# Conditioning blocks in buffers of their own, 24 of them in the mixer's projections, and two eight-product pairs in three of four feed-forward layers

## The chip, the cores and the metric

The kernel runs on one core of a Trainium2 chip. The metric is the device time of one execution, in microseconds (us); less is better.

## What is computed

One inference step of a two-layer (DEPTH 2) diffusion trunk over T = 640 tokens, 128 of context and 512 latent, with D = 1024 channels, all in fp32:

```python
m = silu(cond) @ ada_w[l] + ada_b[l]                  # 9 vectors of D per layer, two streams
x += 0.5 * m[2] * swiglu_a(modulate(norm(x), m[0:2]))
x += m[5] * mixer_l(modulate(norm(x), m[3:5]))        # even l: attention; odd l: retention
x += 0.5 * m[8] * swiglu_b(modulate(norm(x), m[6:8]))
swiglu(h): a, b = split(h @ w13); (silu(a) * b) @ w2  # w13: 1024 x 2*2816, w2: 2816 x 1024
```

So there are four feed-forward networks, FFN 0 to FFN 3, with mixer 0 (neighbourhood and latent attention over one input projection) between FFN 0 and 1, and the retention mixer between FFN 2 and 3. The two streams (context, latent) have conditioning vectors of their own, so each row of `m` is made twice, from two rows silu(cond).

## The kernel before, in words

Channels lie on the 128 partitions, tokens along the free axis. Every fp32 product is made of three matmuls of fp32r parts (high x high, high x low, low x high), so each weight and each activation needs a high part (rounded, on ScalarE, ACT) and a low part (the difference, on VectorE, DVE).

**Weights.** Blocks of 128 x 1024 (512 KB) or 128 x 768 stream from HBM through the ring `raw` of four slots, in the order that `stream_order()` writes out; the SP queue issues them all (L621). ACT and DVE split a block (`split(n)`: L795 or L802, and L1298) into the two slots of `w2` that TensorE (PE) reads.

**Conditioning.** `ada_w` has 16 groups of KD = 8 blocks of 128 x 1024 that are worked during the run, 128 in all (two further groups are worked at the start). For each, DVE makes a reduction with the silu(cond) row of each stream, `crow[:, s, :]` (L1311, two operations of 1024 columns and a read of each accumulator into `acol`). After each group of eight `ada_out` adds the bias and counts `ada_ev`. These blocks go through the same ring (L623, issued by SP). ADA_UP and ADA_DN say after which tile pair and after which of an FFN's closing tiles how many are worked: 48 in FFN 0, 24 in FFN 1, 24 in FFN 2; 32 come one by one in the retention mixer's heads.

**An FFN.** 22 tile pairs f (an up and a gate tile of 128 channels each) in rounds of 6, 6, 6 and 4; after each round eight "down" tiles add the round's share of the product with w2 (L2171, 288 matmuls a round of six). A pair has one of two forms. The eight-product form (f < CLASSIC[q], `first_pairs`) is 96 matmuls of 320 columns (L2054; the first pair of an FFN is L2100). The seven-product form (`seven_products`) makes the 2 x 2 block product in seven passes of 12 matmuls, 84 in all (L2138). It needs sums of weight quarters (on DVE L1438, L1445, L1452, L1458, with low parts in L1472 and L1467, all `left_low` and `left_..._sum`) and, once for an FFN, sums of activation quarters: the T sums (`t_values` L1481 to L1490, `t_high` on ACT, `t_low` L1500 on DVE), made at pair T_PAIR[q]. Between its passes PE waits for banks of PSUM that ACT (L945, copies to `swu`) and DVE (L1612) have to empty.

**Mixer 0.** Its projections are the steps e = 0 to 13, each with one weight block split two steps ahead (L1761) and in the first eight a memset (L1764); then come two memsets of `va_e`, the norms `nvar` (L1769, L1770), a power on GpSimd (POOL), and `diag` (L1335), which PE needs at L2118. The activations `h2`, `qz` and the rest of the mixer fill SBUF otherwise.

**Names.** raw: ring of weight blocks. crow: silu(cond) rows. acol: accumulators. mod: the finished vectors m. swu: copies of PSUM in a seven-product pair. e2s, e2: T sums and their parts. h2: activations, high and low. n: number of a block; u, r: pair within its round, round.

## Time and profile before

| | |
|---|---|
| median of three runs | 3091.01 us (3086.54, 3091.01, 3091.66) |
| the profiled execution's own time | 3088.77 us |
| its span in the trace | 3086.9 us |
| granted TensorE clock over the span, as a share of 2.4 GHz | 0.988 |
| PE busy | 2953.0 us, 96% |
| DVE busy | 2004.9 us, 65% |
| ACT busy | 1135.0 us, 37% |
| DMA | 294.42 MB, mean 95 GB/s |

A share of busy time is a mean over the stages. The page's chain of waits follows back from the last instruction what released what: here 83% of it lies on PE, 8% on DVE. In the views of single instructions a row is the start, the duration, the engine, the line of the kernel and the operation with out<-in; in brackets stands the idle time of that engine just before it, and the instruction or transfer that ended it.

### The profile page before, as it was taken

How to read it: one execution, taken by the hardware profiler on the slowest of the kernel's cores; microseconds unless marked ns; L12 is line 12 of the kernel's file. 1: busy time of each engine (PE TensorE's matmuls, PEld its weight loads, DVE VectorE, ACT ScalarE, POOL GpSimd, SP SyncE). 2: the span in 40 equal slices, each digit the busy share in tenths (PEclk: the TensorE clock that was granted, in tenths of full speed). 3: DMA queues.
4: the chain of work that ended last, by engine and by line, in shares of the span. 5: the costliest groups of instructions: out<-in, count | busy, mean ns of one | idle time of the engine just before them, and what ended most of it. 6: DMA issues, size and time to landing. Idle time of an engine off the chain costs nothing.

```text
span 3086.9 us, 46070 instructions
## 1 busy us (share of the span) xinstructions
PE 2953.0 (96%) x18222; PEld 2719.1 (88%) x18222; DVE 2004.9 (65%) x3616; ACT 1135.0 (37%) x2024; POOL 275.8 (9%) x335
## 2 busy tenths in 40 slices
PE   7999998998999899999899999999999999999998
PEld 3999898988878899998899998778686886899998
DVE  3778878246756787776787776463635545667766
ACT  4223434335455243444343444222212222534433
POOL 1000002011003000003000003030302104100001
PEclk9999999999999999999999999999999999999999
DMA  5453342220102333332334232312223241122221
GB/s 220 137 175 119 112 128 97 81 70 27 42 15 62 124 112 117 97 113 65 123 104 127 94 107 86 123 62 96 96 76 116 77 129 42 43 94 85 78 82 66
DMA packets 87686, 294.42 MB, mean 95 GB/s; under 512 B 10512, under 2 KB 14896, under 8 KB 86704
## 3 DMA queue, kind: packets, MB, share of 16 engines
q1 hardware_dynamic: 80080, 269.70, 27.0%
q10 hardware_dynamic: 6176, 16.54, 1.4%
q0 software_dynamic: 1216, 5.24, 0.5%
q8 instruction: 144, 2.36, 0.3%
q14 instruction: 70, 0.57, 0.1%
HBM read 283.96 MB, written 7.49 MB: 94 GB/s over the span
## 4 chain that ended last, share of the span: by engine, by line
PE 83%; DVE 8%; ACT 3%; issue 2%; POOL 2%; DMA 1%; DVEq 0%; POOLq 0%; ACTq 0%; SPq 0%
PE ps L2138 23%; PE ps L2171 18%; PE ps L2304 12%; PE ps L2039 11%; PE ps L2054 7%; PE ps L2100 2%; PE ps L2576 2%; POOL tmp_q L644 2%; PE ps L2585 2%; PE ps L2361 1%; PE ps L2329 1%; PE ps L2564 1%; PE ps L2344 1%; PE ps L2252 1%; DVE prod L1311 1%
## 5 line engine op out<-in xcount | busy, mean ns | idle before, releaser
L2171 PE MATMUL ps<-g,w 128*128 128x320 f32 x4224 | 625.0, 308 | 0.6 <-DVE x L1422 0.6
L2171 PEld LDWEIGHTS ps<-g,w 128*128 128x128 f32 x4224 | 620.6, 187 | 1.4 <-issue 0.8
L2138 PE MATMUL ps<-h,w 128*128 128x320 f32 x3168 | 497.5, 312 | 40.7 <-ACT swu L945 28.2
L2138 PEld LDWEIGHTS ps<-h,w 128*128 128x128 f32 x3168 | 474.7, 189 | 45.7 <-ACT swu L945 29.3
L1298 DVE TENSOR_TENSOR w<-raw,w 128x1024 fp32r<-128x1024 f32 (+1 forms) x267 | 302.8, 1140 | 223.4 <-ACT w L795 207.0
L2304 PE MATMUL ps<-w,h 128*128 128x512 f32 x1620 | 374.4, 391 | 4.8 <-ACT rv L1234 3.1
L2138 PE MATMUL ps<-e,w 128*128 128x320 f32 x2376 | 370.6, 309 | 0.0
L2304 PEld LDWEIGHTS ps<-w,h 128*128 128x128 f32 x1620 | 302.3, 188 | 70.0 <-issue 6.8
L2138 PEld LDWEIGHTS ps<-e,w 128*128 128x128 f32 x2376 | 355.0, 188 | 0.0
L808 ACT ACTIVATE w<-w2s 128x512 fp32r<-128x512 f32 x264 | 163.4, 631 | 253.4 <-DVE w2s L1445 71.7
L2054 PE MATMUL ps<-h,w 128*128 128x320 f32 x1728 | 254.3, 309 | 0.2 <-DVE w L1298 0.2
L2054 PEld LDWEIGHTS ps<-h,w 128*128 128x128 f32 x1728 | 253.6, 188 | 0.4 <-issue 0.4
L644 POOL TENSOR_TENSOR tmp_q<-tmp_q 128x320 f32<-128x320 f32 (+1 forms) x66 | 80.3, 1217 | 1744.2 <-ACT tmp_q L838 1738.8
L802 ACT ACTIVATE w<-raw 128x768 fp32r<-128x768 f32 (+1 forms) x144 | 130.7, 914 | 266.1 <-PE ps L2171 202.7
L2039 PE MATMUL ps<-h,w 128*128 128x320 f32 (+1 forms) x1440 | 217.2, 311 | 3.1 <-DVE rk L1925 3.1
L2039 PEld LDWEIGHTS ps<-h,w 128*128 128x128 f32 x1440 | 213.0, 188 | 5.5 <-issue 5.1
L1422 DVE SCALAR_TENSOR_TENSOR x<-ps,gate,x 128x128 f32<-128x128 f32 x224 | 112.1, 545 | 162.5 <-PE ps L2171 145.0
L795 ACT ACTIVATE w<-raw 128x1024 fp32r<-128x1024 f32 x123 | 128.5, 1061 | 231.7 <-PE ps L2039 128.2
L1472 DVE TENSOR_TENSOR w<-w2s,w 128x512 fp32r<-128x512 f32 x264 | 179.0, 684 | 1.1
L1311 DVE CUSTOM_DVE_ANT_0 raw<-raw,crow 128x1024 f32<-128x1024 f32 x128 | 158.0, 1235 | 4.4
L1311 DVE CUSTOM_DVE_ANT_0 prod<-raw,crow 128x1024 f32<-128x1024 f32 x128 | 156.0, 1219 | 5.7 <-ACT crow L884 2.0
L813 ACT ACTIVATE w<-raw 128x512 fp32r<-128x512 f32 x198 | 123.4, 625 | 97.4 <-PE ps L2171 72.8
(246 smaller groups left out, 3376.2 us busy)
## 6 DMA issues: line engine op xcount, KB each, us to landing
raw<-in_ws SPq DMA_DIRECT2D x303, 512.0 KB, 3.6
raw<-in_ada SPq DMA_DIRECT2D x128, 512.0 KB, 3.8
raw<-in_ws SPq DMA_DIRECT2D x96, 384.0 KB, 3.2
ada<-in_ada ACTq DMA_DIRECT2D x6, 1024.0 KB, 22.5
rst<-in_state ACTq DMA_DIRECT2D x4, 1024.0 KB, 4.8
out_new_state<-rsx ACTq DMA_DIRECT2D x8, 512.0 KB, 2.6
x<-in_xT SPq DMA_DIRECT2D x4, 640.0 KB, 8.5
ada<-in_ada POOLq DMA_DIRECT2D x2, 1024.0 KB, 16.7
```

Source lines behind the costliest of these rows:

```text
L644: pool.tensor_tensor(acc_sq, acc_sq, new_sq, ALU.add).then_inc(sq_add, 1)
L795: act.activation(w2[:, slot_of(n), 0, :], raw_of("w", n), ACT.Copy).then_inc(wt_hi, 1)
L802: act.activation(w2[:, slot_of(n), 0, 0:cols], raw_of("w", n)[:, 0:cols], ACT.Copy).then_inc(wt_hi, 1)
L808: act.activation(left(q, f, m, 0), left_value(q, f, m), ACT.Copy).then_inc(left_hi, 1)
L1298: dve.tensor_tensor(w2[:, slot, 1, 0:cols], raw_of("w", n)[:, 0:cols], w2[:, slot, 0, 0:cols].bitcast(fp32), ALU.subtract).then_inc(wt_lo, 1)
L1311: dve.tensor_tensor_reduce(raw_of("a", b) if s else prod0, raw_of("a", b), crow[:, s, :], 1.0, 0.0, ALU.mult, ALU.add, acol[:, k, s:s + 1] ...
L1472: dve.tensor_tensor(lo, left_value(q, f, m) if m else quarter(n, 0), hi, ALU.subtract).then_inc(left_lo, 1)
L2039: mm = pe.matmul(pair_half(pr, half, width), w2[:, slot, wi, at:at + cols], rhs(k, ri)[:, half * width:(half + 1) * width], start=(k == 0 ...
L2054: mm = pe.matmul(pair_half(pr, half), w2[:, slot_of(n), wi, k * P:(k + 1) * P], h2[:, k, ri, half * HT:(half + 1) * HT], start=(k == 0 and ...
L2138: mm = pe.matmul(ps[:, 4 * s + bank, 0:HT], w2[:, at // 2, wi, c:c + P], rhs(k, ri), start=start and k + wi + ri == 0, stop=(k == 3 and wi ...
L2171: mm = pe.matmul(pair_half(pr, half), w2[:, slot_of(n), wi, c:c + P], half_of(g2[:, k, ri, :], half), start=k + wi + ri == 0, stop=(k == n ...
L2304: mm = pe.matmul(ps[:, bank_of(t), :], ones_tile(src(k, ri), t), w2[:, slot_of(n), wi, kk * 512:(kk + 1) * 512], start=(k == 0 and ri == 0 ...
```

## The change

The conditioning blocks of the four FFNs and of mixer 0 leave the weight ring. They get two buffers, `cond0` and `cond1` (in mixer 0 the two halves of `cond_em`), and are loaded by the POOL queue (`condition_load`), each once the block two before it has been worked. The buffers come from `prod0`, `fourth` and one of the four `swu` planes: the first row's product now goes to two scraps of 512 columns, so that its reduction is made in two operations and each block takes three, whose sums `ada_out` adds; the fourth T sum is made in place in `tscr`; the second copy of a pair in `swu` is shared by both parities, with a wait for `c22_done` of the pair before. The blocks are distributed anew: 32 in FFN 0, 24 in mixer 0's projections (two after each split of e = 1 to 11 and two after the last memsets), with rows `crow_em` that POOL loads and ACT turns to silu, 24 in FFN 1, 16 in FFN 2. Retention's 32 stay in the ring. Of FFN 0's, 5 stand in its four eight-product pairs and 9 in seven-product pairs (before, 21 and 7), of FFN 1's 6 in seven-product pairs (before, 6 in its four eight-product pairs and 2 in the first seven-product ones), of FFN 2's none in any pair. And the first 4, 2, 2, 2 pairs of the FFNs are eight-product pairs (before: 10, 4, 4, 4), with the T sums at pair 1, 0, 0, 0 (before: 3, 1, 1, 1).

```diff
@@ -40,8 +40,8 @@
-CLASSIC = (10, 4, 4, 4)
-T_PAIR = (3, 1, 1, 1)
+CLASSIC = (4, 2, 2, 2)
+T_PAIR = (1, 0, 0, 0)
@@ -49,9 +49,13 @@
-ADA_UP = [[1, 3, 3, 0, 3, 2, 3, 3, 3, 0, 0, 0, 0, 1, 1, 1, 1, 0, 0, 1, 1, 1],
-          [1, 0, 3, 2, 0, 2] + [0] * 16, [1, 0, 3, 2, 0, 2] + [0] * 16, [0] * FT]
-ADA_DN = [[6, 6, 6, 2], [6, 6, 4, 0], [6, 6, 4, 0], [0] * 4]
+ADA_UP = [[2, 0, 2, 1, 1, 2, 0, 1, 0, 1, 0, 0, 0, 1, 0, 1, 0, 0, 0, 1, 1, 0],
+          [0, 0, 0, 0, 0, 0, 0, 1, 0, 1, 0, 0, 0, 1, 0, 1, 0, 0, 0, 1, 1, 0], [0] * FT, [0] * FT]
+ADA_DN = [[6, 6, 6, 0], [6, 6, 6, 0], [6, 6, 4, 0], [0] * 4]
+ADA_FFN = [sum(ADA_UP[q]) + sum(ADA_DN[q]) for q in range(4)]
+ADA_EM = 3 * KD
+ADA_AT = [0, ADA_FFN[0] + ADA_EM, ADA_FFN[0] + ADA_EM + ADA_FFN[1]]
+ADA_RET = ADA_AT[2] + ADA_FFN[2]
@@ -196,38 +200,14 @@
-    order, made = [], [0, 0]
-
-    def weights(to):
-        order.extend(("w", n) for n in range(made[0], to))
-        made[0] = max(made[0], to)
-
...
+    order, at = [], 0
+    for hd in range(RH):
+        for u in range(8):
+            to = HEADS[hd].gf + u + LEAD + 1
+            order.extend(("w", n) for n in range(at, to))
+            order.append(("a", ADA_RET + 8 * hd + u))
+            at = to
+    order.extend(("w", n) for n in range(at, NBLOCKS))
@@ -306,10 +286,11 @@
-        prod0 = place("prod0", BW, at=diag_at - NLAT * 4)
+        cond1 = place("cond1", BW, at=diag_at - NLAT * 4)
+        unused = [place(f"unused{i}", BW // 2, at=base + i * KD * T * 4) for i in range(2)]
-        colmask = place("colmask", 80)
+        colmask = place("colmask", 80, at=base + BW // 2 * 4)
...
@@ -346,11 +327,12 @@
-        swu = place("swu", 4 * HT, at=f_at + 4 * T * 4).rearrange("p (a i t) -> p a i t", a=2, i=2)
-        fourth = place("fourth", 4 * HT, at=f_at + 5 * T * 4).rearrange("p (k t) -> p k t", k=4)
+        swu = place("swu", 3 * HT, at=f_at + 4 * T * 4).rearrange("p (a t) -> p a t", a=3)
+        cond0 = place("cond0", BW, at=f_at + 4 * T * 4 + 3 * HT * 4)
-        assert f_at + 7 * T * 4 <= crow_at
+        assert f_at + 4 * T * 4 + 3 * HT * 4 + BW * 4 <= crow_at
@@ -367,6 +349,8 @@
+        crow_em = place("crow_em", 2 * BW, at=el[0]).rearrange("p (s c) -> p s c", s=2)
+        cond_em = place("cond_em", 2 * BW, at=e_h).rearrange("p (s c) -> p s c", s=2)
...
@@ -521,6 +506,23 @@
+        def cond_of(b):
+            if b >= ADA_RET:
+                return raw_of("a", b)
+            return cond_em[:, b % 2, :] if ADA_FFN[0] <= b < ADA_AT[1] else (cond0, cond1)[b % 2]
+        def cond_loaded(engine, b):
+            if b >= ADA_RET:
+                loaded(engine, "a", b)
+            else:
+                engine.wait_ge(cond_ld[b % 2], 16 * (b // 2 + 1))
+        def worked(b):
+            return 4 * KD + 3 * b + 3
@@ -615,7 +617,7 @@
                     else:
-                        sp.wait_ge(ada_op, 4 * KD + 2 * m + 2)
+                        sp.wait_ge(ada_op, worked(m))
@@ -678,19 +680,37 @@
-            def row_load():
-                pool.dma_start(crow.rearrange("p s c -> p (s c)"), a["crow"].to_broadcast([P, 2 * BW])
+            def row_load(to):
+                pool.dma_start(to.rearrange("p s c -> p (s c)"), a["crow"].to_broadcast([P, 2 * BW])
+            def condition_load(b):
+                pool.wait_ge(ada_op, worked(b - 2))
+                pool.dma_start(cond_of(b), a["ada"][2 * KD + b]).then_inc(cond_ld[b % 2], 16)
+            def ffn_conditions(q):
+                pool.wait_ge(h_hi, chunk(NORM_BEFORE[q], 1, KD - 1))
+                for b in range(ADA_AT[q], ADA_AT[q] + ADA_FFN[q]):
+                    condition_load(b)
-            row_load()
+            row_load(crow)
+            ffn_conditions(0)
+            pool.wait_ge(wt_free, done(pair_block(0, LAST, ROUNDS[LAST] - 1) + 1))
+            row_load(crow_em)
+            for b in range(2):
+                condition_load(ADA_FFN[0] + b)
+            for b in range(2, ADA_EM):
+                condition_load(ADA_FFN[0] + b)
@@ -699,7 +719,7 @@
-            pool.wait_ge(ada_ev, 8)
+            pool.wait_ge(ada_ev, 9)
...
@@ -909,7 +931,7 @@
-                    row_silu(q + 1)
+                    row_silu(crow, 2 * q + 1)
@@ -933,16 +955,16 @@
                     first_half_high(f - 1, u - 1)
-                if f == CLASSIC[q] + 1:
-                    act.wait_ge(t_lo, t_turn(q, 3))
                 act.wait_ge(left_free, 5 * sg + 1)
-                act.activation(swu[:, s, 0, :], ps[:, 4 * s, 0:HT], ACT.Copy).then_inc(p_copied, 1)
+                act.activation(swu[:, s, :], ps[:, 4 * s, 0:HT], ACT.Copy).then_inc(p_copied, 1)
                 act.wait_ge(left_free, 5 * sg + 2)
-                act.activation(swu[:, s, 1, :], ps[:, 4 * s + 2, 0:HT], ACT.Copy).then_inc(p_copied, 1)
+                if sg:
+                    act.wait_ge(c22_done, sg)
+                act.activation(swu[:, 2, :], ps[:, 4 * s + 2, 0:HT], ACT.Copy).then_inc(p_copied, 1)
@@ -1025,10 +1047,10 @@
             act.wait_ge(h_odd, 16)
-            act.wait_ge(ada_op, 8 * 16)
-            act.wait_ge(ada_ev, 8)
+            act.wait_ge(ada_op, worked(ADA_FFN[0] - 1))
             act.dma_start(ckvr[:, :, 0:PAST], a["cache_ckv"]).then_inc(em_ld2, 16)
+            row_silu(crow_em, 2)
@@ -1298,18 +1320,19 @@
-            def ada_blocks(count):
+            def ada_blocks(count, rows=crow):
-                    loaded(dve, "a", b)
-                    for s in range(2):
-                        dve.wait_ge(ada_op, 4 * KD + 2 * b + s)
-                        dve.tensor_tensor_reduce(raw_of("a", b) if s else prod0, raw_of("a", b), crow[:, s, :], 1.0, 0.0,
-                                                 ALU.mult, ALU.add, acol[:, k, s:s + 1]).then_inc(ada_op, 1)
+                    cond_loaded(dve, b)
+                    for i, (c0, c1, row, to) in enumerate(((0, BW // 2, 0, 0), (BW // 2, BW, 0, 2), (0, BW, 1, 1))):
+                        dve.wait_ge(ada_op, worked(b - 1) + i)
+                        at = cond_of(b)[:, c0:c1]
+                        dve.tensor_tensor_reduce(at if row else unused[b >= ADA_AT[1]], at, rows[:, row, c0:c1], 1.0, 0.0,
+                                                 ALU.mult, ALU.add, acol[:, k, to:to + 1]).then_inc(ada_op, 1)
@@ -1318,9 +1341,10 @@
-                dve.wait_ge(ada_op, j * 16 + 16)
+                dve.wait_ge(ada_op, worked(KD * (j - 1) - 1))
-                dve.tensor_tensor(dst, acol, b.to_broadcast([P, KD, 2]), ALU.add).then_inc(ada_ev, 1)
+                link(dve.tensor_tensor(dst, acol[:, :, 0:2], b.to_broadcast([P, KD, 2]), ALU.add))
+                dve.tensor_tensor(dst[:, :, 0:1], dst[:, :, 0:1], acol[:, :, 2:3], ALU.add).then_inc(ada_ev, 1)
...
@@ -1542,9 +1566,10 @@
                 if f == 0 and q < 2:
-                    dve.wait_ge(crow_done, q + 1)
-                ada_blocks(ADA_UP[q][f])
-                if f + 1 == CLASSIC[q] < FT:
+                    dve.wait_ge(crow_done, 2 * q + 1)
+                if not seven:
+                    ada_blocks(ADA_UP[q][f])
+                else:
@@ -1552,6 +1577,7 @@
                     left_low(q, f + 1, n + 2, 6)
+                    ada_blocks(ADA_UP[q][f])
@@ -1560,13 +1586,13 @@
-                u2, v = swu[:, s, 0, :], swu[:, s, 1, :]
+                u2, v = swu[:, s, :], swu[:, 2, :]
-                    dve.tensor_tensor(tmp_g[:, s, 0:HT], swu[:, s, 0, :], ps[:, 4 * s + 3, 0:HT], ALU.add
+                    dve.tensor_tensor(tmp_g[:, s, 0:HT], swu[:, s, :], ps[:, 4 * s + 3, 0:HT], ALU.add
@@ -1759,9 +1785,14 @@
                 split(n0 + e + LEAD)
+                if e == 1:
+                    dve.wait_ge(crow_done, 2)
+                ada_blocks(2, crow_em)
                     dve.memset(qz[h][64:128] if h % 2 == 0 else qz[h][0:64], 0.0)
+            ada_blocks(2, crow_em)
+            dve.wait_ge(ada_op, worked(ADA_FFN[0] + ADA_EM - 1))
```

SP's instructions, from the first weight block on. `raw<-in_ws` is a weight block, `raw<-in_ada` a conditioning block. Before:

```order
L621 DMA raw<-in_ws 128x1024 x4
L623 DMA raw<-in_ada 128x1024
L621 DMA raw<-in_ws 128x1024 x2
L623 DMA raw<-in_ada 128x1024 x3
L621 DMA raw<-in_ws 128x1024 x2
```

With the change:

```order
L623 DMA raw<-in_ws 128x1024 x12
L623 DMA raw<-in_ws 128x768 x8
L623 DMA raw<-in_ws 128x1024 x12
L623 DMA raw<-in_ws 128x768 x8
L623 DMA raw<-in_ws 128x1024 x12
```

The conditioning blocks are gone from SP's queue up to the retention mixer.

DVE in FFN 1, from the low part of its second pair on. L1530 multiplies a pair's silu with its gate, L1537 makes the low part of the result, L1481 to L1490 (now L1505 to L1514) are the T sums, L1524 a T sum's low part, L1496 and L1462 and on the first work for a seven-product pair. Before:

```order
L1298 TENSOR_TENSOR w2_55<-raw_53,w2_55 128x1024
L1530 TENSOR_TENSOR tmp_g_92<-tmp_s_90,ps 128x640
L1537 TENSOR_TENSOR g2_87<-tmp_g_92,g2_87 128x640
L1311 ISA prod0_60,acol_72<-raw_53,crow_96 128x1024
L1311 ISA acol_72 128x1
L1311 ISA raw_53,acol_72<-raw_53,crow_96 128x1024
L1311 ISA acol_72 128x1
L1298 TENSOR_TENSOR w2_55<-raw_53,w2_55 128x1024 x2
L1481 TENSOR_TENSOR e2s_52<-e2s_52 128x4x320
L1485 TENSOR_TENSOR e2s_52<-e2s_52 128x4x320
L1487 TENSOR_TENSOR e2s_52<-e2s_52 128x4x320
L1490 TENSOR_TENSOR fourth_95<-tscr_88,e2s_52 128x1280
```

With the change:

```order
L1320 TENSOR_TENSOR w2_55<-raw_53,w2_55 128x1024
L1505 TENSOR_TENSOR e2s_52<-e2s_52 128x4x320
L1509 TENSOR_TENSOR e2s_52<-e2s_52 128x4x320
L1511 TENSOR_TENSOR e2s_52<-e2s_52 128x4x320
L1514 TENSOR_TENSOR tscr_90<-tscr_90,e2s_52 128x1280
L1554 TENSOR_TENSOR tmp_g_94<-tmp_s_92,ps 128x640
L1524 TENSOR_TENSOR e2_51<-e2s_52,e2_51 128x4x320
L1561 TENSOR_TENSOR g2_89<-tmp_g_94,g2_89 128x640
L1524 TENSOR_TENSOR e2_51<-e2s_52,e2_51 128x4x320 x2
L1496 TENSOR_TENSOR w2_55<-raw_53,w2_55 128x512
L1462 TENSOR_TENSOR w2s_54<-raw_53 128x512
L1469 TENSOR_TENSOR w2s_54<-w2s_54,raw_53 128x512
```

The conditioning block has left this place, and the T sums stand one pair earlier, ahead of the first pair's product.

DVE at the end of mixer 0's projections, with the names of above, before:

```order
L1298 TENSOR_TENSOR w2_55<-raw_53,w2_55 128x1024
L1764 MEMSET qz7_105 64x640
L1298 TENSOR_TENSOR w2_55<-raw_53,w2_55 128x1024 x3
L1765 MEMSET va_e_106 64x512
L1766 MEMSET va_e_106 64x512
L1769 TENSOR_SCALAR nvar_74<-ps 128x5
L1770 TENSOR_SCALAR nvar_74<-ps 128x5
L1335 TENSOR_TENSOR diag_61<-ident_56,nrs_75 128x640
```

With the change, rows of the first of these steps: the second of its two blocks, its memset and the split of the next step (`unused0` is a scrap of 512 columns, L1334 the reductions, L1320 the low part of a weight block, L1793 the memset):

```order
L1334 ISA unused0_61,acol_74<-cond_em_111,crow_em_110 128x512
L1334 ISA acol_74 128x1
L1334 ISA unused0_61,acol_74<-cond_em_111,crow_em_110 128x512
L1334 ISA acol_74 128x1
L1334 ISA cond_em_111,acol_74<-cond_em_111,crow_em_110 128x1024
L1334 ISA acol_74 128x1
L1793 MEMSET qz0_100 64x640
L1320 TENSOR_TENSOR w2_55<-raw_53,w2_55 128x1024
```

Between two splits, where one memset stood, there are now up to two blocks of three reductions each, and two more stand ahead of `nvar`.

## Rows read from the trace of the kernel before

**Rows 1.** The page: span, and busy time of the engines.

```profile
span 3086.9 us, 46070 instructions
...
PE 2953.0 (96%) x18222; PEld 2719.1 (88%) x18222; DVE 2004.9 (65%) x3616; ACT 1135.0 (37%) x2024; POOL 275.8 (9%) x335
```

**Rows 2.** Waits of PE: waiter, releaser, us in total, times, longest.

```profile
PE ps L2138 <- ACT swu L945: 28.2, 4, 12.3
...
PE ps L2138 <- DVE swu L1612: 12.5, 15, 1.7
```

**Rows 3.** Windows: stretch, length, then busy us of PE, PEld, DVE, ACT, POOL.

```profile
242.60:271.30 28.70, 26.46 (x171) 26.20 (x170) 22.50 (x38) 15.66 (x28) 0.00 (x0) 0.94 0.28 91
313.50:395.30 81.80, 75.29 (x507) 73.97 (x506) 68.40 (x127) 37.78 (x74) 0.00 (x0) 1.00 0.36 122
437.50:491.00 53.50, 50.06 (x338) 49.27 (x337) 45.60 (x83) 25.05 (x47) 0.00 (x0) 1.00 0.43 144
1020.90:1060.20 39.30, 26.92 (x170) 26.39 (x170) 32.26 (x55) 15.22 (x27) 0.00 (x0) 0.83 0.32 110
...
2692.40:2719.80 27.40, 25.20 (x170) 24.68 (x169) 20.93 (x35) 15.01 (x27) 0.00 (x0) 1.00 0.30 90
2762.10:2836.10 74.00, 74.00 (x506) 74.00 (x506) 60.71 (x112) 38.43 (x74) 0.00 (x0) 1.00 0.28 89
```

**Rows 4.** Timeline of PE: start of the sevens in FFN 1 and FFN 3.

```profile
1038.35 3.57 PE L2138 MATMUL ps<-h,w 128*128 128x320 f32 x12 [12.03 <-ACT swu L945]
...
2699.53 2.02 PE L2138 MATMUL ps<-h,w 128*128 128x320 f32 x12 [1.64 <-ACT swu L945]
```

**Rows 5.** Timeline of DVE in FFN 1: before the first seven-product pair.

```profile
1026.52 1.22 DVE L1311 CUSTOM_DVE_ANT_0 prod<-raw,crow 128x1024 f32<-128x1024 f32 x1
...
1038.55 0.69 DVE L1438 TENSOR_TENSOR w2s<-raw 128x512 f32<-128x512 f32 x1 [4.29 <-DMA raw<-in_ws]
```

**Rows 6.** Timeline of DVE in FFN 3: its first four pairs.

```profile
2647.19 1.22 DVE L1298 TENSOR_TENSOR w<-raw,w 128x1024 fp32r<-128x1024 f32 x1 [1.41 <-ACT w L802]
...
2656.00 1.49 DVE L1481 TENSOR_TENSOR e2s<-e2s 128x1280 f32<-128x1280 f32 x1
...
2665.23 0.82 DVE L1530 TENSOR_TENSOR tmp_g<-tmp_s,ps 128x640 f32<-128x640 f32 x1 [3.19 <-ACT tmp_s L903]
...
2684.51 1.89 DVE L1472 TENSOR_TENSOR w<-w2s,w 128x512 fp32r<-128x512 f32 x3
```

**Rows 7.** Timeline of DVE and PE in FFN 0: a pair with a block.

```profile
358.68 0.69 DVE L1438 TENSOR_TENSOR w2s<-raw 128x512 f32<-128x512 f32 x1 [1.34 <-DMA raw<-in_ws]
...
360.95 1.23 DVE L1311 CUSTOM_DVE_ANT_0 raw<-raw,crow 128x1024 f32<-128x1024 f32 x1
...
367.05 3.78 PE L2138 MATMUL ps<-h,w 128*128 128x320 f32 x24 [1.62 <-DVE swu L1612]
```

**Rows 8.** Groups by form: another operation of the same DVE opcode, narrower.

```profile
L1817 DVE CUSTOM_DVE_ANT_0 sb<-ps,bias 128x384 f32<-128x384 f32 x16 | 8.9, 556 | 16.8 <-PE ps L2330 16.8
```

**Rows 9.** Timeline of DVE and PE: end of the projections of mixer 0.

```profile
548.84 1.23 DVE L1298 TENSOR_TENSOR w<-raw,w 128x1024 fp32r<-128x1024 f32 x1
550.14 0.59 DVE L1764 MEMSET qz<- 64x640 f32 x1
...
617.07 0.17 DVE L1769 TENSOR_SCALAR nvar<-ps 128x5 f32<-128x5 f32 x1
...
619.39 0.83 DVE L1335 TENSOR_TENSOR diag<-ident,nrs 128x640 f32<-128x640 f32 x1 [2.09 <-POOL nrs L696]
...
627.96 1.24 PE L2118 MATMUL ps<-diag,ones 128*128 128x320 f32 x4
```

**Rows 10.** DMA issues of POOL: KB each, median us from issue to landing.

```profile
ada<-in_ada POOLq DMA_DIRECT2D x2, 1024.0 KB, 16.7
crow<-in_crow POOLq DMA_DIRECT2D x2, 1024.0 KB, 5.0
rows<-in_rpb POOLq DMA_DIRECT2D x8, 128.0 KB, 2.3
```

More of the change, by code:

```diff
@@ L320, in build @@
         amul = place("amul", 16).rearrange("p (m s) -> p m s", s=2)
-        acol = place("acol", 16).rearrange("p (m s) -> p m s", s=2)
+        acol = place("acol", 24).rearrange("p (m s) -> p m s", s=3)
         gate = place("gate", 16).rearrange("p (m s) -> p m s", s=2)
@@ L448, in build @@
         ada1_load = [sem(f"ada1_load{i}") for i in range(ADA1 // 2)]
+        cond_ld = [sem(f"cond_ld{i}") for i in range(2)]
         ada_rowc, crow_ld, crow_done = sem("ada_rowc"), sem("crow_ld"), sem("crow_done")
@@ L820, in t_high @@
                 else:
-                    act.activation(h2[:, 0:4, 0, HT:T], fourth, ACT.Copy).then_inc(t_hi, 1)
+                    act.activation(h2[:, 0:4, 0, HT:T], tscr, ACT.Copy).then_inc(t_hi, 1)
             def norm_sq(k, nn, ready, h=None):
@@ L880, in norm_tail, with row_silu @@
                         early()
-            def row_silu(count):
+            def row_silu(row, count):
                 act.wait_ge(crow_ld, 16 * count)
-                act.activation(crow, crow, ACT.Silu).then_inc(crow_done, 1)
+                act.activation(row, row, ACT.Silu).then_inc(crow_done, 1)
             def first_pairs(q, r, u):
@@ L1489, in t_values @@
                     low_done(dve, nn, 0, k)
-                dve.tensor_tensor(fourth, tscr, t2, ALU.subtract).then_inc(t_val, 1)
+                dve.tensor_tensor(tscr, tscr, t2, ALU.subtract).then_inc(t_val, 1)
             def t_low(q, v):
```

31 lines of the change are left out of this document (4 added, 27 removed).

## The prediction

> **What bounds the kernel now.** I read the page first. PE is busy for 96% of the span, DVE for 65% [rows 1]. So time leaves only with matmuls, or from the few places where PE waits. The waits of PE then name the place that the change works on: PE stands at the seven-product pairs, 28.2 us in four long waits for ACT's copies into `swu`, and 12.5 us in 15 short ones for DVE's additions there [rows 2]. The list does not say what a wait costs with the slower clock after it, so I read windows that hold nothing but sevens. In FFN 3 six undisturbed pairs take 74.00 us, 12.33 each [rows 3]: 84 matmuls at 0.1467 us, or 1.76 us for twelve. An eight-product pair, 96 matmuls, is 14.08 by the same pitch. Every window less 12.32 a pair gives its stall:
>
> - FFN 0: 4.0 at its first two sevens (28.70), 7.8 in the six of the third round (81.80), 4.2 in the last four (53.50) [rows 3], together 16.1.
> - FFN 1: 14.7 at its first two (39.30) [rows 3], 1.2 at the starts of its later rounds. FFN 2 is alike, 15.1 and 1.1.
> - FFN 3, which works no conditioning blocks: 2.7 at its first two (27.40) [rows 3].
>
> The sum is 50.9 us. What ends each wait is in the timelines. In FFN 1 DVE works a block at 1026.52 and then idles 4.29 us, until a weight block lands; only then, at 1038.55, does it make the first sum for the sevens [rows 5]. SP could not issue this weight earlier: it stood behind conditioning blocks in the ring. PE idles 12.03 us, and its next twelve matmuls take 3.57 us [rows 4], where twelve took 2.02 after a wait of 1.64 in FFN 3 [rows 4]. The granted clock is 0.83 in the first window and 1.00 in the second [rows 3]: after the long wait PE starts at the lower of its two levels (1.2 and 2.4 GHz), which costs 1.6 us. In FFN 0's later pairs one block is worked in a seven. DVE idles 1.34 us for the weight that queued behind it, the block's second half starts at 360.95, and PE then waits 1.62 [rows 7].
>
> **The change, part by part.**
>
> *Twelve pairs change form.* 6 + 2 + 2 + 2 pairs go from 96 to 84 matmuls: 12 x 12 x 0.1467 = 21.1 us off PE, which bounds these stages: **-21.1**.
>
> *The first sevens of FFN 1, 2 and 3.* No block stands before them, and weights are no longer behind blocks in SP's queue. What is left is DVE's own work, which now must fit beside two eight-product pairs. In FFN 3 I walk it: the second pair's split ends at 2648.4 [rows 6]; four T sums of 1.49 (6.0), the product of pair 0 (0.8), a T low part (1.5), pair 0's low part (0.8), two more T low parts (2.9) and seven halves of 0.63 (4.4) [rows 6] end at 2664.8. DVE had pair 1's silu at 2665.23 [rows 6], so the new order has 0.4 to 0.7 us to spare, and the first seven should stall as FFN 3's does now: 2.7 each. With the 1.2 at round starts: FFN 1 3.9, FFN 2 3.9, FFN 3 2.7.
>
> *Blocks in sevens.* A block is now reduced in three operations. One of 1024 columns took 1.23 [rows 7], one of 384 columns in another operation of the same opcode 0.556 [rows 8], so 512 columns should take about 0.69, and the block, with its reads, 2.72 to 2.83 where it was 2.53. In an undisturbed seven DVE is busy 60.71 of 74.00 us [rows 3], that is 2.2 us a pair free. A single block then overshoots by 0.5 to 0.6, of which I charge 0.4, and 1.0 for the second of two neighbouring pairs. Bounds: nothing, and today's 12.0 / 7 = 1.7 for each block of FFN 0's last two windows. Each of FFN 0 and FFN 1 has six such blocks in the later rounds, four alone and two neighbours: 3.0. In FFN 0 the first seven has a block just before and one inside: 2.7 + 2 x 2.8 + 1.6 for the clock = 9.9; two blocks at f = 5, the last pair of a round with less to prepare, 1.0; round starts 1.0: in all 14.9. FFN 1: 3.9 + 3.0 = 6.9. All stalls become 14.9 + 6.9 + 3.9 + 2.7 = 28.4 in place of 50.9: **-22.5**.
>
> *24 blocks in mixer 0.* Today PE runs on without a wait up to 627.96, where it needs `diag` [rows 9]; DVE had that at 619.39 + 0.83, 7.7 us early. Now DVE has more to do than the stretch is long. The first split comes some 2 us later, as ACT first makes silu of two more rows (estimated from 1024 columns at 1.2), so I start at 548.84 [rows 9]. Eight splits with a memset at 1.90 and three at 1.30 (548.84 to 550.14, and 0.59 for the memset [rows 9]): 19.1. 24 blocks at 2.78: 66.7. Three `ada_out` 0.9, one us for the last load, two memsets 1.2: 637.7. From `nvar` to the end of `diag` 3.2 (617.07 to 620.22 [rows 9]): 640.9. PE waits 12.9, then 1.6 for the clock: **+14.5**. Bounds: +10 if a block takes 2.6, and the rival below. The splits for PE stay ahead: the last before `nvar` is done by about 632, and PE gets to it near 636.
>
> *The loads.* A buffer is free from its block's end to its next use, one step of 7.5 us less a block: 4.7 us. POOL's transfers took 2.3 us for 128 KB and 5.0 for 1024 KB [rows 10]; 512 KB lies between, some 3.5, so I cost them at nothing. Cover: if it went, the steps would take the load's time plus 2.75. The end far off is the 16.7 us of 1024 KB at the start [rows 10], when the inputs were in flight too. In the FFNs the blocks are farther apart and have more cover.
>
> *At nothing:* the wait of ACT's second copy for `c22_done` (a pair, 12.3 us, lies between), the missing wait for T low parts, the fourth T sum in place (DVE's work stays the same), 96 transfers fewer in the ring (SP is no limit).
>
> Sum: 3088.8 - 21.1 - 22.5 + 14.5 = 3059.7. The profiled execution, 3088.77, is 2.2 below the median of the three runs and 2.2 above the lowest; I put the forecast one above the sum: **3061**. By the bounds it has its own range, 3053 to 3069.
>
> **Weighed against the trace.** POOL's transfers of 1024 KB took 5.0 us with DVE at work nearby [rows 10], but none was issued while DVE ran reductions end to end, as it now does. The Trainium skill, SBUF — State Buffer, section "SBUF: two separate sides", says that descriptors of a DMA issued by GpSimd can't be written while VectorE runs an operation in a two-port mode, and under "Who interferes with whom" that two-input operations have no such mode. By the first alone each load would land up to one reduction of 1.23 later, 4.7 us, and the sum would stand within 2 us; by several in a row it is the third rival; by the second nothing changes.
>
> **The rivals.**
>
> 1. *DVE, not the ring, makes the wait of a seven with a block.* For it: PE's releaser is DVE in 15 waits [rows 2], and DVE's work grows by 0.2 to 0.3 a block. Against it: the 1.34 us for a weight [rows 7]. Then a single block keeps 1.7: 12 blocks from 6.0 to 20 us, and some 3 more at FFN 0's start: 3061 + 17 = 3078.
> 2. *T sums late.* The margin of the walk is under 0.7 us, and it takes ACT's high parts to be in time. If the first seven of FFN 1, 2 and 3 has to wait for the T sums, each pays about their 6.0 us and 1.6 for the clock: + 23, 3084.
> 3. *Slower than before: POOL's loads.* Place: the eleven steps of mixer 0. From 4.7 us a load sets the step, as load plus 2.75. The gain of 28 us is used up where the twelve rounds are 2.4 us longer each, at a load of some 7.1 us. At 8 us: 12 x 3.25 = 39, and some 2 in the FFNs: 3102. For it: the 16.7 us of rows 10; against it: the 5.0 for double the size, in the same rows.
> 4. *Cheaper.* A block of two short and one long reduction at 2.6, and blocks in sevens free: -4.5 in the mixer, -6 to -11 in FFN 0 and 1: 3047.
>
> That the change doesn't do what it says has no chance of its own: the order shows 144 matmuls fewer and SP's queue without blocks.
>
> **How the numbers follow.** Forecast 0.60, first rival 0.17, second 0.10, third 0.06, fourth 0.07. The range 3046 to 3080 holds the forecast, the first and the fourth rival, and leaves out most of the second and the third. 0.2% is 6.2 us, about what a measurement of this kernel tells from no change. Slower by more than that needs the third rival: 0.05. Within 0.2% end rivals 1 and 2 together, or a mild case of the third: 0.05. Faster: 0.90.
>
> **What would show it.** Right: PE with 18078 matmuls; the windows of the first two sevens in FFN 1 and 2 at 27.4 instead of 39.3, with a granted clock of 1.00; PE's one long wait, some 13 us, at the mixer's `diag` matmul with DVE as releaser, and DVE without gaps in the projections, which start some 12 us earlier than now; POOL's loads at 3 to 5 us. Wrong: a wait for `cond_em` ahead of most reductions in the mixer (third rival); 14 us between the starts of sevens with a block (first); PE stalls of 8 to 10 us at the first sevens (second). The forecast falls if the mixer's wait isn't between 8 and 18 us, since no other term is as large and as new.

## The result, and the profile after

The change made the kernel 1.1% faster: 3057.74 us, the median of four runs (3055.96 to 3058.38), against 3091.34 before (3086.54 to 3093.18). The ratio is 0.9893, with a 95% interval of 0.9876 to 0.9910. The forecast was 3061 with a range of 3046 to 3080. The profiled execution has a span of 3054.1 us where the one before had 3086.9 [rows 1], so 32.8 us are to be found in the trace.

The page of the changed kernel, the lines that answer to [rows 1], and DMA issues, which answer to [rows 10]:

```profile
span 3054.1 us, 46577 instructions
...
PE 2932.0 (96%) x18078; PEld 2697.9 (88%) x18078; DVE 2108.6 (69%) x4080; ACT 1174.5 (38%) x2133; POOL 326.3 (11%) x432
...
raw<-in_ws SPq DMA_DIRECT2D x303, 512.0 KB, 3.7
cond<-in_ada POOLq DMA_DIRECT2D x72, 512.0 KB, 3.9
...
cond_em<-in_ada POOLq DMA_DIRECT2D x24, 512.0 KB, 3.8
```

PE has 144 matmuls fewer (18222 before) and is still busy for 96%. POOL's transfers of 512 KB land after 3.8 to 3.9 us, like SP's.

The waits of PE in the changed kernel (waiter, releaser, us in total, times, longest), which answer to [rows 2]:

```profile
PE ps L2149 <- DVE diag L1359: 13.1, 1, 13.1
...
PE ps L2169 <- DVE swu L1638: 9.2, 8, 5.8
...
PE ps L2169 <- ACT swu L967: 8.3, 4, 2.5
```

The sevens' waits went from 28.2 + 12.5 us to 8.3 + 9.2. The one new entry is `diag`, 13.1 us, once.

Windows of the changed kernel over its sevens (stretch, length, busy us of PE, PEld, DVE, ACT, POOL, granted clock, DMA share, GB/s), which answer to [rows 3]:

```profile
115.10:150.20 35.10, 27.68 (x170) 27.15 (x168) 31.37 (x61) 15.02 (x27) 2.12 (x4) 0.90 0.40 122
309.30:383.90 74.60, 74.31 (x505) 73.91 (x505) 65.37 (x125) 38.10 (x74) 1.05 (x2) 1.00 0.31 104
994.10:1046.10 52.00, 49.81 (x338) 49.29 (x337) 43.09 (x77) 28.29 (x53) 0.00 (x0) 1.00 0.28 87
1438.70:1492.20 53.50, 50.97 (x338) 50.70 (x338) 44.33 (x79) 29.08 (x54) 0.00 (x0) 0.97 0.28 86
2633.10:2686.60 53.50, 50.99 (x337) 50.73 (x336) 44.25 (x79) 29.04 (x54) 0.00 (x0) 0.97 0.28 86
```

The stretches are the first sevens of FFN 0 (two pairs), FFN 0's third round (six), and the first sevens of FFN 1, 2 and 3 (four each). Less 12.32 us a pair, the stalls are 10.5, 0.7, 2.7, 4.2 and 4.2 us. FFN 0's other rounds stall 0.7 and 1.2, FFN 1's later ones 2.6 together, and FFN 2 and 3 have none left in theirs. The sum is 27.0 us, where it was 50.9.

Timeline of PE in the changed kernel: the two waits at FFN 0's first sevens, the wait in mixer 0, and the first sevens of FFN 1 and FFN 2, each with the 42 matmuls that end the norm ahead of it. They answer to [rows 4, 9]:

```profile
122.12 2.02 PE L2169 MATMUL ps<-h,w 128*128 128x320 f32 x12 [1.63 <-ACT swu L967]
...
133.46 6.34 PE L2169 MATMUL ps<-h,w 128*128 128x320 f32 x24 [5.80 <-DVE swu L1638]
...
625.68 2.50 PE L2149 MATMUL ps<-diag,ones 128*128 128x320 f32 x4 [13.07 <-DVE diag L1359]
627.51 8.88 PE L2070 MATMUL ps<-h,w 128*128 128x320 f32 x48
636.23 1.24 PE L2149 MATMUL ps<-diag,ones 128*128 128x320 f32 x4
...
972.48 7.74 PE L2131 MATMUL ps<-h,w 128*128 128x320 f32 x42 [1.17 <-POOL h L680]
...
1001.21 2.03 PE L2169 MATMUL ps<-h,w 128*128 128x320 f32 x12 [1.63 <-ACT swu L967]
...
1418.33 6.42 PE L2131 MATMUL ps<-h,w 128*128 128x320 f32 x42 [1.17 <-POOL h L680]
...
1446.65 3.47 PE L2169 MATMUL ps<-h,w 128*128 128x320 f32 x12 [2.53 <-ACT swu L967]
```

In the mixer PE reaches `diag` and waits 13.07 us; then four matmuls take 2.50 us where they took 1.24 [rows 9], and the 48 behind them 8.88. These are the 48 before the change, with the second `diag` group:

```profile
628.80 7.44 PE L2039 MATMUL ps<-h,w 128*128 128x320 f32 x48
636.08 1.24 PE L2118 MATMUL ps<-diag,ones 128*128 128x320 f32 x4
```

From the first `diag` group to the second it was 8.12 us (627.96 to 636.08) and is 10.55 (625.68 to 636.23), so the lower clock behind this wait costs 2.4 us. In FFN 0 PE waits 1.63 and then 5.80, and the 24 matmuls behind the long wait take 6.34 us where 24 take 3.78 at full clock.

DVE in the changed kernel, the stretch ahead of that wait of 5.80, and in mixer 0 the last two waits for a load and `diag`:

```profile
122.69 0.68 DVE L1334 CUSTOM_DVE_ANT_0 unused<-cond,crow 128x512 f32<-128x512 f32 x1
...
125.30 0.69 DVE L1462 TENSOR_TENSOR w2s<-raw 128x512 f32<-128x512 f32 x1
125.90 0.68 DVE L1334 CUSTOM_DVE_ANT_0 unused<-cond,crow 128x512 f32<-128x512 f32 x1
...
129.72 0.48 DVE L1621 TENSOR_TENSOR swu<-swu,ps 128x320 f32<-128x320 f32 x1
...
132.93 0.48 DVE L1638 TENSOR_TENSOR swu<-swu,ps 128x320 f32<-128x320 f32 x1
...
614.94 0.69 DVE L1334 CUSTOM_DVE_ANT_0 unused<-cond_em,crow_em 128x512 f32<-128x512 f32 x1 [1.16 <-DMA cond_em<-in_ada]
...
618.14 0.69 DVE L1334 CUSTOM_DVE_ANT_0 unused<-cond_em,crow_em 128x512 f32<-128x512 f32 x1 [0.51 <-DMA cond_em<-in_ada]
```

At 122.69 and 125.90 DVE works the blocks of f = 3 and f = 4, with one weight sum between them; only at 129.72 does it come to the first addition into `swu`, and at 132.93 to the one that PE waits for (L1638). In the mixer the blocks run end to end, and the loads hold DVE up for 1.16 us at most.

The account, from the profiled executions:

| | forecast | measured |
|---|---|---|
| twelve pairs of the other form | -21.1 | 144 matmuls less, -21.1 |
| stalls in sevens | 50.9 to 28.4, -22.5 | 50.9 to 27.0, -23.9 |
| mixer 0 | +14.5 | 13.2 + 2.4, +15.7 |
| elsewhere | 0 | -3.5 |
| sum | -29.1 | -32.8 |

In the mixer's row 13.2 is how much later PE starts `diag`, counted from the group before it (27.40 us, from 598.28 on, in place of 14.16). "Elsewhere" can be followed from stage to stage: the norms ahead of FFN 2 and 3 end 1.5 us sooner each (their last 42 matmuls 6.42 and 6.43 us, before 7.95 and 7.96), the first norm starts 0.8 us earlier (65.72 in place of 66.54, and 65.67 in a run that changes nothing ahead of it), and the stretch behind FFN 3's last tile pairs is 0.4 longer.

### The profile page after: what moved, and what is told of

Same layout as the page of the kernel before. It is cut to its first block, busy times and chain, and to the rows that moved or that the text cites. A ratio compares the mean times of both kernels' runs of the same rounds, so it can differ in the third digit from the quotient of the medians.

```text
span 3054.1 us, 46577 instructions
## 1 busy us (share of the span) xinstructions
PE 2932.0 (96%) x18078; PEld 2697.9 (88%) x18078; DVE 2108.6 (69%) x4080; ACT 1174.5 (38%) x2133; POOL 326.3 (11%) x432
## 4 chain that ended last, share of the span: by engine, by line
PE 83%; DVE 8%; ACT 3%; issue 2%; POOL 2%; DMA 1%; DVEq 0%; POOLq 0%; ACTq 0%
PE ps L2169 29%; PE ps L2202 18%; PE ps L2335 12%; PE ps L2070 8%; PE ps L2085 2%; PE ps L2607 2%; POOL tmp_q L646 2%; PE ps L2616 2%; PE ps L2131 1%; PE ps L2392 1%; PE ps L2360 1%; PE ps L2595 1%; DVE unused L1334 1%; PE ps L2283 1%; PE ps L2375 1%
## 5 line engine op out<-in xcount | busy, mean ns | idle before, releaser
L2202 PE MATMUL ps<-g,w 128*128 128x320 f32 x4224 | 624.7, 309 | 0.0
L2202 PEld LDWEIGHTS ps<-g,w 128*128 128x128 f32 x4224 | 620.5, 188 | 0.6
L2169 PE MATMUL ps<-h,w 128*128 128x320 f32 x3744 | 585.8, 311 | 17.5 <-DVE swu L1638 9.2
L2169 PEld LDWEIGHTS ps<-h,w 128*128 128x128 f32 x3744 | 561.2, 189 | 21.5 <-DVE swu L1638 11.3
L2169 PE MATMUL ps<-e,w 128*128 128x320 f32 x2808 | 437.3, 309 | 0.0
L2169 PEld LDWEIGHTS ps<-e,w 128*128 128x128 f32 x2808 | 418.6, 188 | 0.0
L1320 DVE TENSOR_TENSOR w<-raw,w 128x1024 fp32r<-128x1024 f32 (+1 forms) x243 | 274.6, 1132 | 169.6 <-ACT w L817 151.9
L830 ACT ACTIVATE w<-w2s 128x512 fp32r<-128x512 f32 x312 | 193.1, 630 | 276.4 <-DVE w2s L1469 84.0
L2070 PEld LDWEIGHTS ps<-h,w 128*128 128x128 f32 x1440 | 214.4, 189 | 5.6 <-issue 5.5
L1496 DVE TENSOR_TENSOR w<-w2s,w 128x512 fp32r<-128x512 f32 x312 | 211.7, 684 | 1.2
L2070 PE MATMUL ps<-g,w 128*128 128x320 f32 x960 | 144.4, 312 | 2.3 <-DVE g L2039 1.5
L2070 PEld LDWEIGHTS ps<-g,w 128*128 128x128 f32 x960 | 143.0, 190 | 3.1 <-issue 2.0
L690 POOL DMA_DIRECT2D cond<-in_ada x72 | 38.5, 534 | 976.5 <-DVE acol L1334 976.5
L2131 PE MATMUL ps<-h,w 128*128 128x320 f32 x576 | 99.5, 324 | 24.8 <-DVE h L1401 9.4
```

Of the source, the lines that this page charges most:

```text
L830: act.activation(left(q, f, m, 0), left_value(q, f, m), ACT.Copy).then_inc(left_hi, 1)
L1320: dve.tensor_tensor(w2[:, slot, 1, 0:cols], raw_of("w", n)[:, 0:cols], w2[:, slot, 0, 0:cols].bitcast(fp32), ALU.subtract).then_inc(wt_lo, 1)
L1496: dve.tensor_tensor(lo, left_value(q, f, m) if m else quarter(n, 0), hi, ALU.subtract).then_inc(left_lo, 1)
L2070: mm = pe.matmul(pair_half(pr, half, width), w2[:, slot, wi, at:at + cols], rhs(k, ri)[:, half * width:(half + 1) * width], start=(k == 0 ...
L2131: mm = pe.matmul(pair_half(pr, h), w2[:, slot_of(n), wi, k * P:(k + 1) * P], half_of(h2[:, k, ri, :], h), start=(k == 0 and wi == 0 and ri ...
L2169: mm = pe.matmul(ps[:, 4 * s + bank, 0:HT], w2[:, at // 2, wi, c:c + P], rhs(k, ri), start=start and k + wi + ri == 0, stop=(k == 3 and wi ...
```

## The experiments

Two questions were left by the result. Is it the ring that made sevens with blocks slow, or DVE's work? And is the price of the mixer really one of too many blocks? The first four runs ask both.

**The form alone, blocks in the ring.** In the kernel before:

```diff
-CLASSIC = (10, 4, 4, 4)
-T_PAIR = (3, 1, 1, 1)
+CLASSIC = (10, 2, 2, 2)
+T_PAIR = (3, 0, 0, 0)
...
-          [1, 0, 3, 2, 0, 2] + [0] * 16, [1, 0, 3, 2, 0, 2] + [0] * 16, [0] * FT]
+          [1, 1, 1, 2, 1, 2] + [0] * 16, [1, 1, 1, 2, 1, 2] + [0] * 16, [0] * FT]
```

> The kernel before with the form alone: two eight-product pairs in FFN 1, 2 and 3 (T sums at pair 0), FFN 0 as it was, conditioning blocks still in the weight ring, those of FFN 1 and 2 at 1, 1, 1, 2, 1, 2 in the first six pairs. Theory (blocks in the ring make a seven late): six pairs of 12 matmuls less are -10.6, but each of the two FFNs now has six blocks in sevens at 1.7 to 2 us and more where two stand together, so its first round stalls 12 to 20 us where it stalled 14.7: 3075 to 3090. Rival (only DVE's own work counts, the ring does not): six blocks at 0.3 to 0.6 and a first stall near 4, some 6 us a round: 3091 - 10.6 - 17 = 3063.

Measured: 3099.8 us against 3090.6, ratio 1.0027 (1.0018 to 1.0037): slower than before, with 72 matmuls less. That is beyond the theory's end and far from the rival's 3063. The window of FFN 1's first four sevens, and DVE's rows in it:

```profile
993.60:1065.80 72.20, 54.01 (x338) 52.88 (x337) 61.31 (x109) 29.06 (x55) 0.00 (x0) 0.88 0.34 116
```

```profile
1009.86 0.69 DVE L1438 TENSOR_TENSOR w2s<-raw 128x512 f32<-128x512 f32 x1 [4.29 <-DMA raw<-in_ws]
...
1024.87 0.69 DVE L1438 TENSOR_TENSOR w2s<-raw 128x512 f32<-128x512 f32 x1 [2.54 <-DMA raw<-in_ws]
```

The window is 72.20 us for 49.28 of matmuls: a stall of 22.9 where it was 14.7. DVE idles 4.29 us for a weight block, the very number of [rows 5], and again 2.54 later. So with the blocks in the ring and six of them in the first sevens of FFN 1 and of FFN 2, the other form is worth nothing; its 10.6 us were given back in the same rounds. How the 22.9 divide is not shown: DVE waits 6.8 us for weights here (4.3 before), and its six blocks are 15.2 us where four sevens leave it some 8.8 (an estimate, from 2.53 a block and the 60.71 of 74.00 us of [rows 3]). No run has these places with buffers of their own.

**Four eight-product pairs in every FFN.** In the changed kernel:

```diff
-CLASSIC = (4, 2, 2, 2)
-T_PAIR = (1, 0, 0, 0)
+CLASSIC = (4, 4, 4, 4)
+T_PAIR = (1, 1, 1, 1)
```

> The changed kernel with four eight-product pairs in every FFN (T sums at pair 1), so FFN 1, 2 and 3 have two more each. By the matmuls alone +10.6. Theory: in FFN 2 and 3 the first seven waits 2.5 and then runs at the lower clock because the T sums fill the two pairs before it; with four pairs it waits 1.6 at full clock, which gives back 1.5 each: 3057.7 + 10.6 - 3 = 3065. Rival (the T sums are not what is late): 3068.

Measured: 3068.0 (3067.5 to 3068.7), +10.3 on the changed kernel. The time is the rival's, but the first sevens of FFN 1, 2 and 3 all wait 1.63 us at full clock, as the theory had it, and what is missing lies elsewhere. PE's wait in the mixer, which this edit does not touch, was longer:

```profile
PE ps L2149 <- DVE diag L1359: 16.0, 1, 16.0
```

It is 16.0 where the changed kernel had 13.1, and DVE's waits for `cond_em` in the mixer are 6.1 us in total where they were 2.8. The two differences are the same 3 us. Besides, the norm ahead of FFN 2 ended 1.5 us later than in the changed kernel (its last 42 matmuls took 7.96 us in place of 6.42).

**18 blocks in the mixer.** In the changed kernel:

```diff
-ADA_UP = [[2, 0, 2, 1, 1, 2, 0, 1, 0, 1, 0, 0, 0, 1, 0, 1, 0, 0, 0, 1, 1, 0],
+ADA_UP = [[2, 0, 2, 1, 1, 2, 0, 1, 0, 1, 0, 1, 0, 1, 0, 1, 0, 1, 0, 1, 0, 1],
...
-ADA_DN = [[6, 6, 6, 0], [6, 6, 6, 0], [6, 6, 4, 0], [0] * 4]
+ADA_DN = [[7, 7, 7, 1], [6, 6, 6, 0], [6, 6, 4, 0], [0] * 4]
...
-ADA_EM = 3 * KD
+ADA_EM = 18
...
-                ada_blocks(2, crow_em)
+                if e <= 9:
+                    ada_blocks(2, crow_em)
...
-            ada_blocks(2, crow_em)
```

> The changed kernel with 18 conditioning blocks in mixer 0 (steps 1 to 9) and six more in FFN 0: two in seven-product pairs, three in its closing tiles, one at its end. Theory (DVE's blocks alone make PE's wait of 13.1 us for diag, 24 of them being some five too many): DVE is done 16.7 us earlier, the wait and the 1.4 us of lower clock behind it are gone, and the six blocks cost 1 to 3 us in FFN 0: 3044 to 3047. Rival (something else in that stretch holds diag, the silu rows or the loads): the wait stays above 8 us and the time above 3052.

Measured: 3040.1 (3039.4 to 3042.0), and 3041.2 (3037.4 to 3042.3) when run again: 17 us below the changed kernel, ratio to before 0.9835 (0.9819 to 0.9851). That is below the theory's 3044 to 3047 too. PE's wait for `diag` is gone from its list of waits. `diag` is done at 605.33 and PE comes to it at 610.88, and DVE waits for PE instead:

```profile
DVE cqr L1807 <- PE ps L2149: 5.2, 1, 5.2
```

The six blocks moved cost FFN 0 nothing, where the theory charged 1 to 3 us: its four down rounds start 0.1, 0.1, 0.5 and 1.6 us earlier than in the changed kernel, the last because no two sevens with a block are neighbours any more. A block between two sevens that have none costs 0.3 us or less.

**FFN 0's blocks at f = 3 and 4 moved to f = 0 and 5.**

```diff
-ADA_UP = [[2, 0, 2, 1, 1, 2, 0, 1, 0, 1, 0, 0, 0, 1, 0, 1, 0, 0, 0, 1, 1, 0],
+ADA_UP = [[3, 0, 2, 0, 0, 3, 0, 1, 0, 1, 0, 0, 0, 1, 0, 1, 0, 0, 0, 1, 1, 0],
```

> The changed kernel with the two blocks ahead of and in FFN 0's first seven (f = 3 and 4) moved to f = 0 and f = 5: 3, 0, 2, 0, 0, 3. Theory: the wait of 5.8 us and the 2.7 of lower clock behind it go, the last pair of the round has room for its third block: -7 to -8.5, 3050. Rival: three blocks ahead of the down tiles make those late instead, and the time stays within 2 us of 3057.

Measured: 3061.0 (3060.0 to 3062.3), slower than the changed kernel by 3.3. Timeline of PE:

```profile
130.01 3.79 PE L2169 MATMUL ps<-h,w 128*128 128x320 f32 x24 [0.57 <-DVE swu L1638]
...
148.23 3.57 PE L2169 MATMUL ps<-h,w 128*128 128x320 f32 x12 [5.63 <-DVE swu L1638]
```

The wait of 5.80 is 0.57 now, as expected, but the three blocks at f = 5 make one of 5.63 inside that pair, with the lower clock behind it. The rival had the place one step off: not the down tiles, the pair itself. The third block at f = 0 makes PE wait 1.8 us for weights (`w`, L1320) besides, so FFN 0's down tiles start 1.4 us later than in the changed kernel. The mixer's wait is longer again, 14.6 in place of 13.1.

**Twice the loads.** In the changed kernel, in `condition_load`:

```diff
+                if ADA_FFN[0] <= b < ADA_AT[1]:
+                    pool.dma_start(cond_of(b), a["ada"][2 * KD + b]).then_inc(cond_again[b % 2], 16)
+                    pool.wait_ge(cond_again[b % 2], 16 * ((b - ADA_FFN[0]) // 2 + 1))
                 pool.dma_start(cond_of(b), a["ada"][2 * KD + b]).then_inc(cond_ld[b % 2], 16)
```

> The changed kernel with every conditioning block of mixer 0 transferred twice by POOL, one after the other (the first is waited for, then the second). It prices the slower side that was forecast: a step takes a load plus 2.75 us once the load is longer than some 4.7. Two transfers of 3.8 and the wait between are about 8 us for a load, so a step takes 10.8 where it took 7.4: +34 to +40, 3092 to 3098, with DVE waiting for cond_em ahead of most blocks. Rival (POOL's loads overlap enough, the DVE work alone sets the step): under +10, 3068.

Measured: 3115.3 (two runs, 3112.9 and 3117.8), +57.6 on the changed kernel, ratio to before 1.0084 (1.0064 to 1.0104). The waits of PE:

```profile
PE ps L2153 <- DVE diag L1363: 31.2, 1, 31.2
PE ps L2074 <- DVE w L1324: 19.3, 7, 5.6
```

The mechanism of the slower side holds, and its price was too low. A step took 12.0 us and not 10.8: the transfers landed after 4.5 us in the median where 3.8 had been put. (POOL's queue also takes the waits of both buffers in turn; what part that has was not separated.) The splits of PE's weights stand behind the waiting blocks on DVE, so PE lost 19.3 us for weights besides the 31.2 at `diag`. Its busy time rose from 2932.0 to 2955.7 us for the same matmuls, with a granted clock of 0.79 in the mixer (540 to 700 us). With single loads PE doesn't wait for weights there.

**Two operations for a block.** In the changed kernel:

```diff
-                    for i, (c0, c1, row, to) in enumerate(((0, BW // 2, 0, 0), (BW // 2, BW, 0, 2), (0, BW, 1, 1))):
+                    for i, (c0, c1, row, to) in enumerate(((0, BW, 0, 0), (0, BW, 1, 1))):
...
-                        dve.tensor_tensor_reduce(at if row else unused[b >= ADA_AT[1]], at, rows[:, row, c0:c1], 1.0, 0.0,
+                        dve.tensor_tensor_reduce(at, at, rows[:, row, c0:c1], 1.0, 0.0,
```

> The changed kernel with the first row's reduction in one operation of 1024 columns, written into the block's own buffer (so the second row reduces the product instead of the block: the conditioning vectors differ from the reference's). Every block takes two operations again. Theory: a block costs 2.53 in place of 2.82, so PE's wait in mixer 0 is 24 x 0.29 = 7 us shorter, less what the loads then hold DVE up: 6 to 9 us in place of 13.1, and the sevens with a block lose their last 0.3: 3049 to 3053. Rival (the loads set the pace of the mixer's blocks): the wait stays above 11 and the time above 3055.

Measured: 3049.9 (3049.9 to 3050.8), 7.8 below the changed kernel's time; but the ratio to the kernel before, taken beside it, is 0.9873 where the change has 0.9893, which is 6 us. The span in the trace is 6.0 us shorter. PE's wait in the mixer is 9.64 us, not the 6 the blocks alone would give: DVE's waits for loads there rose from 2.8 to 4.0 us, and in the last steps they take back part of what shorter blocks give. FFN 0 gave 2.4 us: its last full down round starts at 381.55 in place of 383.90. So the halving of the first row's product, the price of freeing a buffer, costs 6 to 8 us as the blocks stand.

**FFN 0's first eight at 3, 0, 3, 0, 0, 2**, with 18 blocks in the mixer.

> The kernel with 18 blocks in the mixer, and FFN 0's first eight at 3, 0, 3, 0, 0, 2, so that none stands just ahead of or in the first seven, and the last pair of the round keeps two. Theory (the backlog of DVE at the second seven comes from the two blocks at f = 3 and 4, 5.6 us): the wait of 5.8 us and the lower clock behind it go; the third block at f = 2 makes the first seven later by about one us, and the two at f = 5 may show as 2.8: 3033 to 3036. Rival (the third block at f = 2 comes through in full, with the lower clock): 3039 to 3042.

Measured: 3038.8 (3036.4 to 3040.0), which can't be told from the 3040.1 (and, run again, 3041.2) without it. The 5.80 is gone, but the first seven waits 3.34 with the lower clock behind it, the last pair 1.28, and PE waits 1.8 us for weights (`w`, L1320). It is the rival's case in the main.

**The singles where the kernel before has them.**

```diff
-ADA_UP = [[2, 0, 2, 1, 1, 2, 0, 1, 0, 1, 0, 0, 0, 1, 0, 1, 0, 0, 0, 1, 1, 0],
+ADA_UP = [[2, 0, 2, 1, 1, 2, 0, 0, 0, 0, 0, 0, 0, 1, 1, 1, 1, 0, 0, 1, 1, 0],
```

> The changed kernel with FFN 0's singles at f = 13, 14, 15, 16, 19 and 20, where the kernel before has them. There each cost 1.2 to 1.7 us of PE's time. Theory (most of that was the weight block behind the conditioning block in the ring): with their own buffers the overshoot of DVE alone is left, 2.8 less 2.2 of room, adding up over neighbours: 0.3 for the first and 0.6 to 0.8 for each that follows one, some 3 us in all where the placing of the change pays 1.4, 3059. Rival (DVE sets it, the ring does not): 1.3 to 2.0 each, 9 us, 3064 or more.

Measured: 3059.9 (3058.7 to 3060.5). The window of FFN 0's third round, and PE's waits in it:

```profile
308.35:384.90 76.55, 74.85 (x507) 73.92 (x505) 69.89 (x138) 37.43 (x74) 2.12 (x4) 1.00 0.36 115
```

```profile
344.28 3.78 PE L2169 MATMUL ps<-h,w 128*128 128x320 f32 x24 [0.42 <-DVE swu L1638]
...
357.29 3.78 PE L2169 MATMUL ps<-h,w 128*128 128x320 f32 x24 [0.43 <-DVE swu L1638]
...
370.72 3.78 PE L2169 MATMUL ps<-h,w 128*128 128x320 f32 x24 [0.85 <-DVE swu L1638]
```

The same four pairs with a block stalled 7.8 us before (81.80 [rows 3]) and stall 2.6 here (76.55 less 73.92), though each block takes DVE 0.3 us longer. So about two thirds of a seven's stall with a block was the ring, and a third is DVE's overshoot. In the change this round has two such pairs, with one between them, and the stall is 0.7.

**Three eight-product pairs in FFN 2 and 3**, with 18 blocks in the mixer (`CLASSIC = (4, 2, 3, 3)`).

> The kernel with 18 blocks in the mixer, and three eight-product pairs in FFN 2 and 3 (T sums at pair 0 still), so one more each. By the matmuls +3.5. Theory (the T sums' chain ends 0.9 us late there and brings the lower clock): the first seven waits 1.6 at full clock, -2.5 each: 3040.1 + 3.5 - 5.0 = 3038.6. Rival: the first seven's wait is its own preparation, whatever stands before: 3043.6.

Measured: 3040.9 (3039.8 to 3042.7), no difference that can be told. The waits did what the theory says, 1.63 us at full clock in both FFNs:

```profile
1404.38 6.43 PE L2131 MATMUL ps<-h,w 128*128 128x320 f32 x42 [1.17 <-POOL h L680]
...
1445.88 2.02 PE L2169 MATMUL ps<-h,w 128*128 128x320 f32 x12 [1.63 <-ACT swu L967]
```

But the gain had been put too high. With two pairs and 18 blocks the stall of these sevens was 4.3 us in each FFN, since the twelve matmuls behind the wait took 2.8 and 3.2 us there and not 3.5, and it is 2.7 now: 3.2 us for both, against 3.5 us of matmuls.

The traces show when the first seven comes late. Ahead of each of these FFNs stand the 42 matmuls that end the norm. In the changed kernel's timeline above they took 7.74 us ahead of FFN 1, and its first seven waits 1.63; ahead of FFN 2 they took 6.42, and its first seven waits 2.53 and starts at the lower clock (twelve matmuls in 3.47). In the profiled executions there are 32 such places with two pairs ahead of the sevens and no blocks there, and each reads so: 7.7 to 9.2 us and then 1.63, or 6.4 us and then 2.5. The granted clock over the norm's last 20 us is 0.91 in the one case (0.83 in the three longest) and 1.00 in the other. PE that comes at full clock comes 1.5 us sooner to a DVE that needs its 16.3 us for the T sums and the first halves all the same, so it is all given back: the 42 matmuls and the stall make 7.74 + 2.72 in FFN 1 and 6.42 + 4.24 in FFN 2.

**One block in FFN 0's first seven and none ahead**, at 2, 0, 3, 0, 1, 2, and then at 2, 1, 2, 0, 1, 2; both with 18 in the mixer.

> The kernel with 18 blocks in the mixer, FFN 0's first eight at 2, 0, 3, 0, 1, 2: one block in the first seven and none ahead of it, three at f = 2. Theory (DVE's backlog at the second seven is the sum of the blocks at f = 3 and 4): the wait of 5.8 shrinks by 2.8 to some 3, and with it most of the 2.7 of lower clock; the third block at f = 2 makes the first seven some 1.7 later, with the lower clock, as in the run before: 3035 to 3039. Rival: 3040, the block only moves the wait.

> As the one before, with the block at f = 1, the pair of the T sums, instead of a third at f = 2: 2, 1, 2, 0, 1, 2. Theory: DVE has about 14.1 - 10.4 - 4.1 = -0.4 us of room in that pair, so the block's 2.8 is handed to f = 2, which has 4.4 less 5.6 itself: the first seven comes 1.5 to 3 us late, 3036 to 3040. Rival (the T sums late bring the next pair's splits late): PE waits for w in an eight-product pair, 3041 or more.

Measured: 3040.7 (3038.9 to 3044.0) and 3038.6 (3034.7 to 3040.3). Timelines of PE, the first of the two and then the second:

```profile
125.00 3.57 PE L2169 MATMUL ps<-h,w 128*128 128x320 f32 x12 [3.35 <-ACT swu L967]
```

```profile
122.52 2.02 PE L2169 MATMUL ps<-h,w 128*128 128x320 f32 x12 [1.63 <-ACT swu L967]
...
131.24 5.33 PE L2169 MATMUL ps<-h,w 128*128 128x320 f32 x24 [3.18 <-DVE swu L1638]
```

In the second the wait of 5.80 is 3.18, 2.6 less for one block less in the backlog, and the first seven is as before: DVE's idle time at f = 2 and 3 took the moved block. In the first a third block at f = 2 makes the first seven wait 3.35 at the lower clock. By the traces the second placing saves 2.2 to 2.6 us in FFN 0; by the times it isn't told from the 3040.1 and 3041.2.

> The kernel with 18 blocks in the mixer again, beside the three above on the same chip, so that differences of 1 to 3 us can be read: 3040 +- 1.5.

This last run, 3041.2, is the second of the two named.

## Why the prediction was right

- *Twelve pairs, -21.1.* Right by count; the windows show sevens at 12.3 us in the places of eight-product pairs. In FFN 1 and 2 the form needed the blocks out of the way: six pairs of it alone, in FFN 1 to 3, lost 9 us. No run has the buffers with the pairs' old forms, so what the buffers give by themselves was not measured.
- *First sevens of FFN 1, 2 and 3.* Forecast 2.7 each and 1.2 at later round starts. FFN 1 is 2.7. FFN 2 and 3 are 4.2, with nothing at their later rounds. The step that was off is the walk's end, "the new order has 0.4 to 0.7 us to spare": the chain itself took what was forecast (16.4 us by the sum, 16.3 measured, 978.40 to 994.74 in FFN 1), but the time at which it is needed was read from an FFN whose norm ended at the lower clock. At full clock the need comes 1.5 us sooner, and the spare turns into 0.9 us of lateness. It is the second rival in small, 1.5 us for an FFN in place of 7.6. The 1.5 us saved in each of the two norms pay for it; they stand in the account under elsewhere.
- *Blocks in sevens.* A block takes 2.70 us to its end and 2.84 to the next, as forecast from widths. Single ones cost 0.3 and the second of two neighbours some 0.9, charged at 0.4 and 1.0. In FFN 0's first sevens 9.9 and 1.0 were forecast, 10.5 measured, in the form that was forecast: two blocks' backlog and the lower clock.
- *The first rival*, that DVE and not the ring makes the wait: wrong in the main by the singles put back, 2.6 us for four where it asks for 7; a third of the stall is DVE's.
- *Mixer 0, +14.5.* It is +15.7. PE's wait was forecast at 12.9 and is 13.07, but the clock behind it at 1.6 and is 2.4, since the 48 matmuls after `diag` run at the lower clock too. DVE's walk held since blocks, splits and memsets have fixed durations. That it comes within 0.2 us is in part luck: the loads cost 1.8 us more than the one that was put down, and the rest of the walk some 1.6 less. That the blocks' number is what decides was shown by taking six away.
- *The loads.* Costed at nothing with one us for the last. DVE's waits for them add up to 2.8 us in the changed kernel, and in three other profiled executions of the same mixer to 3.0, 4.2 and 6.1, with PE's wait at 14.0, 14.6 and 16.0. So they do set the last steps, where no split or memset lies between two blocks. POOL's blocks took 3.8 to 3.9 us in the median, SP's 3.7, with DVE running reductions end to end in the mixer (the first two 7.6 and 9.4, issued long before their use). This agrees with the second rule that was cited from the Trainium skill's page SBUF — State Buffer ("Who interferes with whom"). What stands beside these loads on DVE are reductions, low parts and memsets, so the first rule wasn't put to a test.
- *The third rival*: its mechanism is real and its place was right; with every load made twice it gives 3115, more than the 3102 that was worked out for loads of 8 us.

By the account the sum was 3.7 us high: 1.4 in the sevens and 3.5 elsewhere, most of it the two norms' 3.1, less 1.2 that the mixer cost more than forecast. That the sum is off by no more owes something to luck, since the mixer's overrun hides a part of the rest. One reading in the prediction is loose: of the "four long waits" of 28.2 us [rows 2] two are long, 12.03 and 12.31, and the others are 2.24 and 1.64; no term hangs on it.

## What to carry to other kernels

A resource that streams in order makes everything behind a slow consumer wait, so taking the slow consumer's loads out of it can be the condition for another change, which alone would lose: here six pairs of the new form lost 9 us by themselves, and with the buffers twelve gave their 21. Work moved under another engine's stretch is free up to the room there and costs its full length beyond; count the room in blocks (here 18 were free, and 24 cost 15.7 us) and place the rest where the stretches are still open. Two neighbours add up what one alone absorbs, so spread work in steps of one and leave a step empty.

## What was not expected of the hardware

How fast PE arrives goes with the side of a wait on which the lower clock falls. Ahead of FFN 2 the same 42 matmuls took 7.95 us before the change and 6.42 after, and with the change's order in that place too 7.96 in a run with 18 blocks in the mixer. With two pairs ahead of the sevens, whenever they took 6.4 us the wait behind was 2.5 us and the next twelve matmuls took 2.8 to 3.5 us; whenever they took 7.7 us or more the wait was 1.63 and the twelve took 2.02. With four pairs ahead the wait was 1.63 after either, and with three it was 1.63 after 6.4. Why the clock rises ahead of one norm and not of another is left open. Also left open is what makes the mixer's loads wait 2.8 us in one execution and 6.1 in another.
